# An expert's gather as two rounded-format matmuls, high part and exact rest, in place of one fp32 matmul

## The chip, the cores and the metric

The kernel runs on one core of one Trainium2 chip. The metric is device time in microseconds for one launch; the time before is the median of three runs. The program times each launch as a whole, while the profile comes from one profiled execution.

## The reference

Two residual layers over 256 tokens of width 1024. Layer 0 is a gated linear recurrence beside a dilated attention, then a dense SwiGLU. Layer 1 is a differential attention, then a mixture of experts, and this last stage is what matters here:

```
logits = (xt @ router)                      # 256 tokens x 8 experts
top_v, top_i = lax.top_k(logits, 2)
gates = jax.nn.softmax(top_v, axis=-1)
for e in range(8):
    h = jax.nn.silu(xt @ w1[e]) * (xt @ w3[e])      # 1024 -> 2816
    y = y + dense_gate[:, e:e + 1] * (h @ w2[e])    # 2816 -> 1024
```

Each expert has 34.6 MB of fp32 weights; about a quarter of the tokens choose it.

## The kernel before, in words

All large matmuls are made of three products in a rounded fp32 format that the program calls F32R (and the profile fp32r): a number is split into its high part, rounded to that format, and the exact rest, and hi·hi + hi·lo + lo·hi is summed in PSUM. Weights come in tiles of 1408, 1536 or 1024 columns into eight raw buffers. For each tile ScalarE writes the high part into one of four `whi` buffers (`split_hi`, line 279), VectorE subtracts it from the raw tile to give `wlo` (`split_lo`, line 286), and TensorE runs the three products (`tile_products`, lines 305 to 307). The order on every engine is written out by hand; semaphores join them. SyncE loads a raw buffer again when its `wlo` is done.

The experts run one after the other. For expert n VectorE makes a one-hot matrix `pick` (256 tokens x 128 seats, in two halves of 128 tokens; `pick_tokens`, line 1130) that says which token sits in which seat. TensorE's `gather(n)` (line 1578) then multiplies the tokens with it. For each of KD = 8 chunks of the width and each of NT = 2 halves of the tokens there is one matmul whose stationary operand is 128 tokens x 128 features of `xn` and whose moving operand is the 128 columns of `pick`. These give the expert's input, turned, in PSUM banks 4 and 5. Behind them `gather` transposes `pick` (line 1588, needed to scatter the result back) and multiplies it with the gates (line 1590). ScalarE and VectorE split the gathered input into `xe_hi` and `xe_lo` (`gather_hi`, line 743; `gather_lo`, line 1139), which the expert's up blocks take as stationary operands. `xn` is a plain fp32 copy of x, made once by ScalarE on line 736, because VectorE scales x itself afterwards (line 1218).

`gather(0)` stands on the way into the first expert. The other seven are issued in the middle of the preceding expert, behind its up block 2 (GATHER_AFTER). The up blocks before and behind them need nothing of the gather.

Ahead of `gather(0)` VectorE has, in this order: a copy for the router (line 1098), three `split_lo` of the first expert's tiles, the copy of the router's logits out of PSUM (line 1101), the chain of small operations that ranks them (to line 1128), and `pick_tokens(0, 0)`. TensorE meanwhile computes the logits (line 1565) and, for the seats, a few matmuls of 8 columns (lines 1571 to 1575).

Of the kernel before, what the change touches and what calls it, by code (L numbers as in the profile page):

```python
# [15 lines left out]
ALU = mybir.AluOpType  # L16
ACT = mybir.ActivationFunctionType
AX_X = mybir.AxisListType.X
F32 = mybir.dt.float32
F32R = mybir.dt.float32r  # L20
# [3 lines left out]
P = 128  # L24
S, D = 256, 1024
NT = S // P
# [6 lines left out]
NE = 8  # L33
# [20 lines left out]
G_DN = [[(3, NB)] * 4, [(3, NB), (3, NB), (2, NB), (2, NB)]]  # L54
# [53 lines left out]
def trunk(nc, a, c, out):  # L108

    with ExitStack() as ctx:  # L110
        sem = lambda name: ctx.enter_context(nc.semaphore(name))
# [6 lines left out]
        def at(name, shape, dt=F32, offset=None):  # L118
            size = int(np.prod(shape[1:])) * (1 if dt == U8 else 4)
            here = cur[0] if offset is None else offset  # L120
            if offset is None:
                cur[0] = here + (size + 31) // 32 * 32
            assert here + size <= top, (name, here + size, top)
            return nc.alloc_sbuf_tensor_at(name, shape, dt, offset=here), here + (size + 31) // 32 * 32

        def own(name, shape, dt=F32):
            return at(name, shape, dt)[0]
# [4 lines left out]
        x = own("x", [P, NT, D])  # L132
        xT_at = cur[0]
# [3 lines left out]
        ident, earlier, slots = small[:, 0, :], small[:, 1, :], small[:, 2, :]  # L137
# [11 lines left out]
        gains, after_gains = at("gains", [P, 2, D], F32, phase)  # L149
# [4 lines left out]
        ropeT, _ = at("ropeT", [P, 2, 512], F32, o)  # L154
# [35 lines left out]
        sq0, on0 = four_heads(expE[0]), four_heads(qk2[0])  # L190

        xn, m2 = at("xn", [P, NT, D], F32, after_gains)
        xe_hi, m3 = at("xe_hi", [P, KD, P], F32R, m2)
        xe_lo, m4 = at("xe_lo", [P, KD, P], F32R, m3)
        h_e, m5 = at("h_e", [P, FF], F32, m4)
        hTe_hi, m6 = at("hTe_hi", [P, KF, P], F32R, m5)
        hTe_lo, m7 = at("hTe_lo", [P, KF, P], F32R, m6)
        silu_e, m8 = at("silu_e", [P, 2, NU], F32, m7)
        pick, m9 = at("pick", [P, NT, P], F32, m8)  # L200
        put_next, m10 = at("put_next", [P, S], F32R, m9)
        put, m11 = at("put", [P, S], F32R, m10)
        y_hi, m12 = at("y_hi", [P, D], F32R, m11)
        y_lo, m13 = at("y_lo", [P, D], F32R, m12)
        xT_f, m14 = at("xT_f", [P, KD, S], F32, m5)
        route, m16 = at("route", [P, 12, NT, NE], F32, m13)
        cmp, m17 = at("cmp", [P, 2, NT, NE, NE], F32, m16)
        ones, m19 = at("ones", [P, P], F32, m17)
        seat, m20 = at("seat", [P, NT, 2 * NE], F32, m19)
        gate_col, m21 = at("gate_col", [P, NT], F32, m20)  # L210
        slot_gate, m22 = at("slot_gate", [P, 2], F32, m21)
        more, m23 = at("more", [P, 1], I32, m22)

        late = [at(f"late{j}", [P, kc * n], F32, where)[0] for j, ((kc, n), where) in
                enumerate(zip(G_DN[1], (xT_at, xT_at + 6144, xT_at + 12288, m23)))]

        psum = ctx.enter_context(nc.psum_tensor("psum", [P, 8, 512], F32))

# [22 lines left out]
        rope2_pool = sem("rope2_pool")  # L242
        lam_x = sem("lam_x")
        c_s, c_mx, c_e, c_a, c_tp, c_te, c_av = (sem(n) for n in ("c_s", "c_mx", "c_e", "c_a", "c_tp", "c_te", "c_av"))
        rt_in, bf_in, rx_act, rx_dve, m_lg, m_sel, m_ex, m_d, m_pos, more_set, xn_set = (
            sem(n) for n in ("rt_in", "bf_in", "rx_act", "rx_dve", "m_lg", "m_sel", "m_ex", "m_d", "m_pos", "more_set", "xn_set"))
        m_pick, m_ga, m_ga_hi, m_ga_lo, m_put_r, m_gt, m_cur = (
            sem(n) for n in ("m_pick", "m_ga", "m_ga_hi", "m_ga_lo", "m_put_r", "m_gt", "m_cur"))
        m_silu, m_h, m_tp, m_thi, m_tlo, m_yhi, m_ylo, m_sc, m_acc = (
# [6 lines left out]
        def by_bank(xT, b):  # L256

            return xT[:, 4 * (b % 2):4 * (b % 2) + 4, (b // 2) * P:(b // 2 + 1) * P]
# [22 lines left out]
        def split_lo(dve, q, par, shapes, js=range(GT), in_late=False):  # L281
            for j in js:
                kc, n = shapes[j]
                dve.wait_ge(hi_done, 2 * GT * q + GT * par + j + 1)
                src = late[j] if in_late else raw[GT * par + j]
                nc.vector.tensor_tensor(wlo[j][:, 0:kc * n], src[:, 0:kc * n],  # L286
                                        whi[j][:, 0:kc * n].bitcast(F32), ALU.subtract).then_inc(lo_done, 1)
# [38 lines left out]
        def dn_src(w2, half, part):  # L326
            return [w2[:, k0:k0 + kc, half * NB:(half + 1) * NB] for k0, (kc, _) in zip(DN_K0[part], G_DN[part])]
# [9 lines left out]
        def dn_src_e(e, half, part):  # L337
            return [m_w2[:, bass.ds(e, 1), k0:k0 + kc, half * NB:(half + 1) * NB].rearrange("p e k n -> p (e k) n")
                    for k0, (kc, _) in zip(DN_K0[part], G_DN[part])]

        TURNS = [(0, 4, 6, 3), (4, 4, 7, 4), (8, 4, 6, 5), (12, 4, 7, 6), (16, 3, 6, 7), (19, 3, 3, None)]
        TURN_AFTER = {after: g for g, (_, _, _, after) in enumerate(TURNS) if after is not None}
        GATHER_AFTER = 2

# [15 lines left out]
        def q_moe(n):  # L362

            return Q_MOE + 6 * n
# [186 lines left out]
        def _(act):  # L551
# [181 lines left out]
            for b in range(3):  # L733
                act.wait_ge(t_ps, 20 + b + 1)
                nc.scalar.copy(by_bank(xT_f, b), psum[:, 4 + b, :].rearrange("p (k s) -> p k s", s=P)).then_inc(rx_act, 1)
            nc.scalar.copy(xn[:], x[:]).then_inc(xn_set, 1)
            act.wait_ge(m_d, 1)
            nc.scalar.activation(route[:, 4], route[:, 3], ACT.Exp).then_inc(m_ex, 1)

# [69 lines left out]
        def _(dve):  # L809
            n_link = [0]  # L810

            def link(ins):
                n_link[0] += 1
                ins.then_inc(dve_link, 1)
                dve.wait_ge(dve_link, n_link[0])
# [161 lines left out]
            for t in range(NT):  # L977
                ins = nc.vector.tensor_tensor(proj[:, t, 512:1024].rearrange("p (h c) -> p h c", h=BH),
                                              psum[:, 6 + t, :].rearrange("p (h c) -> p h c", h=BH),
                                              rinv[:, t, :, None].broadcast_to([P, BH, BD]), ALU.mult)  # L980
# [116 lines left out]
            dve.wait_ge(t_ps, 24)  # L1097
            nc.vector.tensor_copy(by_bank(xT_f, 3), psum[:, 7, :].rearrange("p (k s) -> p k s", s=P)).then_inc(rx_dve, 1)
            split_lo(dve, q_moe(0), 0, G_UP, js=(1, 2, 3))
            dve.wait_ge(m_lg, 1)  # L1100
            link(nc.vector.tensor_copy(route[:, LG], psum[:, 0, 0:NT * NE].rearrange("p (t e) -> p t e", e=NE)))

# [143 lines left out]
        def _(pe):  # L1246
# [127 lines left out]
            for b in range(4):  # L1374
                for kk in range(2):
                    for t in range(NT):
                        col = QB + (2 * b + kk) * P
                        ins = nc.tensor.transpose(psum[:, b, kk * S + t * P:kk * S + t * P + P], proj[:, t, col:col + P], ident)
# [4 lines left out]
            for t in range(NT):  # L1383
                for h in range(AH):
                    dst = psum[:, 6 + t, h * AD:(h + 1) * AD]
                    v = [proj[:, tt, VA + h * AD:VA + (h + 1) * AD] for tt in range(NT)]
                    nc.tensor.matmul(dst, ATd[:, t, h, :], v[t], start=True, stop=False)
                    ins = nc.tensor.matmul(dst, ATo[:, h, 1 - t, :], v[1 - t], start=False, stop=True)
# [170 lines left out]
            for t in range(NT):  # L1559
# [4 lines left out]
                for k in range(KD):  # L1564
                    ins = nc.tensor.matmul(psum[:, 0, t * NE:(t + 1) * NE], xT_f[:, k, t * P:(t + 1) * P], router[:, k, :],
                                           start=(k == 0), stop=(k == KD - 1))
# [7 lines left out]
            for t in range(NT):  # L1574
                ins = nc.tensor.matmul(psum[:, 2, 0:NE], ones[:], route[:, SEL, t, :], start=(t == 0), stop=(t == NT - 1))
            ins.then_inc(m_pos, 1)

            def gather(n):

                pe.wait_ge(m_pick, n + 1)  # L1580
                for k in range(KD):
                    for t in range(NT):
                        ins = nc.tensor.matmul(psum[:, 4 + k // 4, (k % 4) * P:(k % 4 + 1) * P],  # L1583
                                               xn[:, t, k * P:(k + 1) * P], pick[:, t, :], start=(t == 0), stop=(t == NT - 1))
                    if k % 4 == 3:
                        ins.then_inc(m_ga, 1)
                for t in range(NT):
                    ins = nc.tensor.transpose(psum[:, 6, 2 * P + t * P:3 * P + t * P], pick[:, t, :], ident)
                for t in range(NT):
                    ins = nc.tensor.matmul(psum[:, 6, 0:1], pick[:, t, :], gate_col[:, t:t + 1],  # L1590
                                           start=(t == 0), stop=(t == NT - 1))
                ins.then_inc(m_gt, 1)

# [27 lines left out]
            def expert(n, last):  # L1621

                q0 = q_moe(n)
                for b in range(1, UB):
                    block_e(n, b)
                    if b == GATHER_AFTER:
                        pe.wait_ge(m_acc, 2 * n + 1)
                        if not last:
                            gather(n + 1)
                    if b in TURN_AFTER:  # L1630
                        g = TURN_AFTER[b]
                        pe.wait_ge(m_h, 8 * n + b + 2)
                        if g == 0 and not last:
                            pe.wait_ge(m_put_r, 2 * n + 4)
                        if g >= 2:
                            pe.wait_ge(m_tlo, 6 * n + g - 1)
                        turn_hidden_e(n, g)
# [18 lines left out]
                scatter(n, 1)  # L1656

            pe.wait_ge(xn_set, 1)
            gather(0)
            pe.wait_ge(more_set, 1)  # L1660
            first_block(0)
# [33 lines left out]
```

## Time and profile before

| | |
|---|---|
| median of 3 runs | 1432.34 us (1428.77 to 1434.25) |
| profiled execution, first to last instruction | 1432.0 us |
| TensorE (PE) busy | 1340.4 us, 94% |
| weight loads (PEld) busy | 1221.9 us, 85% |
| VectorE (DVE) busy | 1095.1 us, 76% |
| ScalarE (ACT) busy | 841.0 us, 59% |
| gather matmuls (line 1583) | 256 records, 32.1 us |
| chain that ended last | TensorE 86%, VectorE 9% |

For the profiled execution only its span is given, 1432.0 us; no time of its own stands beside it. The span is 0.3 us under the median, so a sum made against the span is carried over to the median as it is. A record's duration on TensorE includes the time the pipeline takes to fill and empty, so records overlap: the pace of a row of matmuls is the distance between their starts, not the duration of one. Line 1583 has 128 matmuls in the program (8 experts x 8 chunks x 2 halves) and 256 records: an fp32 matmul appears as two records, each with a weight load of its own. The weight loads and matmuls of the rounded format appear as one record each.

### The profile page before, as it was taken

What the parts mean: (1) busy time and instruction counts of PE and PEld (TensorE: products, weight loads), DVE (VectorE), ACT (ScalarE), POOL (GpSimd) and SP (SyncE); (2) the same over time, 40 slices, a digit from 0 to 9 for tenths busy, and PEclk for the clock granted to TensorE, in tenths of its full rate; (3) what the DMA queues carried; (4) which work ended last, traced back from release to release, by engine and by line L of the source; (5) the groups of instructions that cost most, each with busy time, mean ns of one, the idle gap of its engine ahead of it and who ended that gap; (6) DMA issues with size and microseconds to landing.
All of it is one profiled execution on the core that took longest, in us unless ns stands there. A gap on an engine that the chain in (4) does not pass through costs nothing.

```text
span 1432.0 us, 20794 instructions
## 1 busy us (share of the span) xinstructions
PE 1340.4 (94%) x7430; PEld 1221.9 (85%) x7430; DVE 1095.1 (76%) x1056; ACT 841.0 (59%) x884; POOL 117.3 (8%) x91
## 2 busy tenths in 40 slices
PE   6997898999898976799999999999999999999995
PEld 5887787999686865699899899898998998998994
DVE  4777646444455995669889889989989888898987
ACT  3555333433333463267768767768667677687772
POOL 1044201000001922100000000000000000000001
PEclk9998878999998997799999999999999999999998
DMA  9552025665345531769999999999999999999980
GB/s 331 184 191 68 1 87 175 183 198 188 118 118 178 166 125 25 240 237 329 344 331 347 358 327 346 364 321 342 360 330 346 365 326 347 330 346 355 370 305 31
DMA packets 227056, 359.02 MB, mean 251 GB/s; under 512 B 8400, under 2 KB 155984, under 8 KB 226880
## 3 DMA queue, kind: packets, MB, share of 16 engines
q1 hardware_dynamic: 225344, 351.50, 71.9%
q0 software_dynamic: 1664, 6.88, 1.4%
q8 instruction: 30, 0.49, 0.2%
q14 instruction: 18, 0.15, 0.0%
HBM read 357.30 MB, written 1.05 MB: 250 GB/s over the span
## 4 chain that ended last, share of the span: by engine, by line
PE 86%; DVE 9%; issue 2%; ACT 1%; POOL 1%; DMA 1%; SPq 0%; DVEq 0%; ACTq 0%
PE psum L305 25%; PE psum L307 24%; PE psum L306 24%; DVE wlo L286 3%; PE psum L1583 2%; PE psum L1597 1%; PE psum L1423 1%; DMA raw<-in_ev_w_in 1%; DVE x L837 1%; PE psum L1256 1%; PE psum L1359 1%; PE psum L1339 1%; PE psum L1407 1%; PE psum L1273 1%; PE psum L1399 1%
## 5 line engine op out<-in xcount | busy, mean ns | idle before, releaser
L286 DVE TENSOR_TENSOR wlo<-raw,whi 128x1408 fp32r<-128x1408 f32 (+2 forms) x500 | 794.6, 1608 | 229.4 <-ACT whi L279 224.6
L279 ACT CAST whi<-raw 128x1408 fp32r<-128x1408 f32 (+2 forms) x500 | 661.6, 1328 | 343.5 <-PE psum L307 312.8
L305 PE MATMUL psum<-whi,xe_hi 128*128 128x352 f32 x1024 | 332.4, 325 | 1.3 <-DVE mv L1215 1.3
L307 PE MATMUL psum<-whi,xe_lo 128*128 128x352 f32 x1024 | 330.6, 323 | 0.0
L306 PE MATMUL psum<-wlo,xe_hi 128*128 128x352 f32 x1024 | 330.4, 323 | 0.0
L305 PEld LDWEIGHTS psum<-whi,xe_hi 128*128 128x128 f32 x1024 | 192.4, 188 | 2.0 <-issue 1.4
L305 PE MATMUL psum<-whi,xT_hi 128*128 128x352 f32 (+1 forms) x512 | 186.3, 364 | 8.3 <-DVE wlo L286 6.1
L306 PEld LDWEIGHTS psum<-wlo,xe_hi 128*128 128x128 f32 x1024 | 192.4, 188 | 0.6
L307 PEld LDWEIGHTS psum<-whi,xe_lo 128*128 128x128 f32 x1024 | 192.4, 188 | 0.0
L306 PE MATMUL psum<-wlo,xT_hi 128*128 128x352 f32 (+1 forms) x512 | 185.2, 362 | 0.0
L307 PE MATMUL psum<-whi,xT_lo 128*128 128x352 f32 (+1 forms) x512 | 184.7, 361 | 0.0
L305 PE MATMUL psum<-whi,hTe_hi 128*128 128x512 f32 x352 | 140.6, 399 | 0.0
L306 PE MATMUL psum<-wlo,hTe_hi 128*128 128x512 f32 x352 | 139.3, 396 | 0.0
L307 PE MATMUL psum<-whi,hTe_lo 128*128 128x512 f32 x352 | 139.2, 395 | 0.0
L305 PEld LDWEIGHTS psum<-whi,xT_hi 128*128 128x128 f32 x512 | 98.2, 192 | 20.7 <-issue 6.7
L307 PEld LDWEIGHTS psum<-whi,xT_lo 128*128 128x128 f32 x512 | 98.3, 192 | 10.6
L306 PEld LDWEIGHTS psum<-wlo,xT_hi 128*128 128x128 f32 x512 | 98.3, 192 | 10.1
L451 POOL TENSOR_SCALAR ln_rs<-mv 128x1 f32<-128x1 f32 x8 | 4.9, 612 | 1086.4 <-DVE mv L830 1086.1
L307 PEld LDWEIGHTS psum<-whi,hTe_lo 128*128 128x128 f32 x352 | 66.2, 188 | 15.9
L306 PEld LDWEIGHTS psum<-wlo,hTe_hi 128*128 128x128 f32 x352 | 66.2, 188 | 15.3
L305 PEld LDWEIGHTS psum<-whi,hTe_hi 128*128 128x128 f32 x352 | 66.2, 188 | 15.2
L762 ACT ACTIVATE silu_e<-psum 128x352 f32<-128x352 f32 x64 | 29.7, 464 | 37.6 <-PE psum L307 37.6
(244 smaller groups left out, 1305.3 us busy)
## 6 DMA issues: line engine op xcount, KB each, us to landing
raw<-in_od_w SPq DMA_DIRECT2D x256, 704.0 KB, 6.1
raw<-in_od_w SPq DMA_DIRECT2D x94, 768.0 KB, 6.2
raw<-in_ev_w SPq DMA_DIRECT2D x32, 704.0 KB, 4.2
raw<-in_ev_w_in SPq DMA_DIRECT2D x32, 512.0 KB, 5.4
raw<-in_od_w SPq DMA_DIRECT2D x30, 512.0 KB, 6.1
raw<-in_od_w_in SPq DMA_DIRECT2D x24, 512.0 KB, 3.8
raw<-in_ev_w SPq DMA_DIRECT2D x12, 768.0 KB, 4.5
raw<-in_ev_w_out SPq DMA_DIRECT2D x8, 512.0 KB, 4.4
```

The costliest lines, as they stand in the source:

```text
L279: nc.scalar.copy(whi[j][:, 0:kc * n], src[:, 0:kc * n]).then_inc(hi_done, 1)
L286: nc.vector.tensor_tensor(wlo[j][:, 0:kc * n], src[:, 0:kc * n], whi[j][:, 0:kc * n].bitcast(F32), ALU.subtract).then_inc(lo_done, 1)
L305: nc.tensor.matmul(ps, hi[:, k, t0:t0 + P], w_h, start=(k == first_k), stop=False)
L306: nc.tensor.matmul(ps, hi[:, k, t0:t0 + P], w_l, start=False, stop=False)
L307: last = nc.tensor.matmul(ps, lo[:, k, t0:t0 + P], w_h, start=False, stop=(k == last_k))
L762: nc.scalar.activation(silu_e[:, b % 2, :], psum[:, 2 * (b % 2), 0:NU], ACT.Silu).then_inc(m_silu, 1)
L837: ins = nc.vector.tensor_tensor(v, v, gains[:, 0, :], ALU.mult)
L1256: ins = nc.tensor.transpose(psum[:, 4 + 2 * t + kb, kk * P:(kk + 1) * P], src(4 * kb + kk, t), ident)
L1273: ins = nc.tensor.matmul(ps, lo[:, k, t * P:(t + 1) * P], w_h, start=False, stop=(k == last_k))
L1339: nc.tensor.matmul(dst, lf_hi[:, t, d, h * AD:(h + 1) * AD], m, start=True, stop=False)
L1359: ins = nc.tensor.matmul(dst, k_[:, ts * P:(ts + 1) * P], q_[:, tt * P:(tt + 1) * P], start=True, stop=True)
L1583: ins = nc.tensor.matmul(psum[:, 4 + k // 4, (k % 4) * P:(k % 4 + 1) * P], xn[:, t, k * P:(k + 1) * P], pick[:, t, :], start=(t == 0), sto ...
```

## The change

`xn` becomes two tiles in the rounded format, `xn_hi` (ScalarE's copy on line 736 now writes it) and `xn_lo` (a new subtraction on VectorE, x minus `xn_hi`, 2048 elements in each of 128 partitions). `pick` is held in the rounded format, in which 0 and 1 are exact. `gather` does two matmuls, with `xn_hi` and `xn_lo`, where it did one in fp32. The transposes and the gate matmuls read `pick` as fp32 as before. `cmp` moves to another place in memory, and so does the last of the `late` tiles. TensorE waits once for `xn_lo` before `gather(0)`.

```diff
-        xn, m2 = at("xn", [P, NT, D], F32, after_gains)
+        xn_hi, m2 = at("xn_hi", [P, NT, D], F32R, after_gains)
...
-        pick, m9 = at("pick", [P, NT, P], F32, m8)
+        pick, m9 = at("pick", [P, NT, P], F32R, m8)
...
-        cmp, m17 = at("cmp", [P, 2, NT, NE, NE], F32, m16)
-        ones, m19 = at("ones", [P, P], F32, m17)
+        cmp, _ = at("cmp", [P, 2, NT, NE, NE], F32, m14)
+        ones, m19 = at("ones", [P, P], F32, m16)
...
+        xn_lo, m24 = at("xn_lo", [P, NT, D], F32R, m23)
...
-            nc.scalar.copy(xn[:], x[:]).then_inc(xn_set, 1)
+            nc.scalar.copy(xn_hi[:], x[:]).then_inc(xn_set, 1)
...
             split_lo(dve, q_moe(0), 0, G_UP, js=(1, 2, 3))
+            dve.wait_ge(xn_set, 1)
+            nc.vector.tensor_tensor(xn_lo[:], x[:], xn_hi[:].bitcast(F32), ALU.subtract).then_inc(xn_rest, 1)
             dve.wait_ge(m_lg, 1)
...
                 for k in range(KD):
+                    dst = psum[:, 4 + k // 4, (k % 4) * P:(k % 4 + 1) * P]
                     for t in range(NT):
-                        ins = nc.tensor.matmul(psum[:, 4 + k // 4, (k % 4) * P:(k % 4 + 1) * P],
-                                               xn[:, t, k * P:(k + 1) * P], pick[:, t, :], start=(t == 0), stop=(t == NT - 1))
+                        nc.tensor.matmul(dst, xn_hi[:, t, k * P:(k + 1) * P], pick[:, t, :], start=(t == 0), stop=False)
+                        ins = nc.tensor.matmul(dst, xn_lo[:, t, k * P:(k + 1) * P], pick[:, t, :], start=False, stop=(t == NT - 1))
...
-                    ins = nc.tensor.transpose(psum[:, 6, 2 * P + t * P:3 * P + t * P], pick[:, t, :], ident)
+                    ins = nc.tensor.transpose(psum[:, 6, 2 * P + t * P:3 * P + t * P], pick[:, t, :].bitcast(F32), ident)
...
-                    ins = nc.tensor.matmul(psum[:, 6, 0:1], pick[:, t, :], gate_col[:, t:t + 1],
+                    ins = nc.tensor.matmul(psum[:, 6, 0:1], pick[:, t, :].bitcast(F32), gate_col[:, t:t + 1],
...
             pe.wait_ge(xn_set, 1)
+            pe.wait_ge(xn_rest, 1)
             gather(0)
```

## Rows read from the trace of the kernel before

**Rows 1.** The page: engine, busy us, share of the span, instructions.

```profile
PE 1340.4 (94%) x7430; PEld 1221.9 (85%) x7430; DVE 1095.1 (76%) x1056; ACT 841.0 (59%) x884; POOL 117.3 (8%) x91
```

**Rows 2.** Waits, 634 to 1248 us: who waited for whom, us, times, longest.

```profile
ACT whi L279 <- PE psum L307: 118.1, 164, 2.0
DVE wlo L286 <- ACT whi L279: 71.4, 129, 4.1
ACT silu_e L762 <- PE psum L307: 30.0, 49, 0.6
```

**Rows 3.** Stretches: length, busy per engine, granted clock, DMA share, GB/s.

```profile
634.00:1248.00 614.00, 614.00 (x3574) 575.12 (x3573) 535.65 (x442) 445.89 (x414) 0.00 (x0) 1.00 0.98 344
...
605.20:611.02 5.82, 5.82 (x33) 5.82 (x34) 0.80 (x2) 0.58 (x1) 0.00 (x0) 0.61 0.00 1
...
600.00:605.00 5.00, 2.30 (x10) 2.21 (x10) 3.19 (x19) 0.22 (x1) 0.00 (x0) 0.50 0.92 304
```

**Rows 4.** Timeline around one later gather: start, length, engine, line, operation.

```profile
737.00 3.74 PE L1583 MATMUL psum<-pick,xn 128*128 128x128 f32 x32
...
740.57 0.38 PE L1588 MATMUL psum<-small,pick 128*128 128x128 f32 x2
740.68 0.53 PEld L1590 LDWEIGHTS psum<-gate_col,pick 128*128 128x128 f32 x4
```

**Rows 5.** Timeline of TensorE ahead of the first gather.

```profile
601.24 0.60 PE L1571 MATMUL psum<-route,small 128*128 128x8 f32 x2 [2.76 <-DVE route L1113]
...
602.54 1.00 PE L1575 MATMUL psum<-route,ones 128*128 128x8 f32 x4
605.20 5.98 PE L1583 MATMUL psum<-pick,xn 128*128 128x128 f32 x32 [1.66 <-DVE gate_col L1133]
611.02 0.38 PE L1588 MATMUL psum<-small,pick 128*128 128x128 f32 x2
```

**Rows 6.** Single lines: duration ns minimum/median/maximum, first and last start, forms.

```profile
L1583 PEld LDWEIGHTS psum<-pick,xn x256: 187/192/333, 605.2 to 1244.4; 128*128 128x128 f32 x128
...
L1339 PEld LDWEIGHTS psum<-lev,xT_hi x64: 186/188/333, 113.3 to 148.3; 128*128 128x128 f32 x64
L1339 PE MATMUL psum<-lev,xT_hi x64: 276/280/583, 113.3 to 148.4; 128*128 128x256 f32 x64
...
L1597 PEld LDWEIGHTS psum<-small,h_e x176: 137/139/143, 647.9 to 1384.6; 128*128 128x128 f32 x176
...
L1575 PE MATMUL psum<-route,ones x4: 361/361/361, 602.5 to 603.2; 128*128 128x8 f32 x4
```

**Rows 7.** Timeline, matmuls of 256 columns in the rounded format, first and last.

```profile
116.06 0.41 PE L1339 MATMUL psum<-lev,xT_hi 128*128 128x256 f32 x1
...
117.13 0.41 PE L1340 MATMUL psum<-lev,xT_lo 128*128 128x256 f32 x1
...
147.00 0.28 PE L1339 MATMUL psum<-lev,xT_hi 128*128 128x256 f32 x1
...
148.53 0.28 PE L1340 MATMUL psum<-lev,xT_lo 128*128 128x256 f32 x1
```

**Rows 8.** Timeline, the same format at 512 columns, first and last of 20.

```profile
579.64 0.39 PE L1271 MATMUL psum<-whi,xT_hi 128*128 128x512 f32 x1
...
583.95 0.39 PE L1272 MATMUL psum<-wlo,xT_hi 128*128 128x512 f32 x1
```

**Rows 9.** Groups by line and form, TensorE: busy us, mean ns, idle before.

```profile
L305 PE MATMUL psum<-whi,xe_hi 128*128 128x352 f32 x1024 | 332.4, 325 | 1.3 <-DVE mv L1215 1.3
L305 PE MATMUL psum<-whi,hTe_hi 128*128 128x512 f32 x352 | 140.6, 399 | 0.0
```

**Rows 10.** Timeline of ScalarE, VectorE and TensorE where the new subtraction goes.

```profile
593.72 1.90 ACT L736 COPY xn<-x 128x2048 f32<-128x2048 f32 x1
...
596.24 3.15 DVE L286 TENSOR_TENSOR wlo<-raw,whi 128x1408 fp32r<-128x1408 f32 x2
...
597.70 0.79 PE L1565 MATMUL psum<-router,xT_f 128*128 128x8 f32 x3
...
599.31 0.17 DVE L1101 COPY route<-psum 128x16 f32<-128x16 f32 x1
```

**Rows 11.** Lines of VectorE with the nearest operations: count, busy us, mean ns.

```profile
L910 DVE TENSOR_TENSOR xT_lo<-sA,xT_hi 128x1024 fp32r<-128x1024 f32 x2 | 4.2, 2128 | 0.9 <-ACT xT_hi L606 0.9
L1132 DVE TENSOR_SCALAR pick<-small,seat 128x128 f32<-128x128 f32 x16 | 3.8, 280 | 0.0
L896 DVE TENSOR_TENSOR sB<-sB,lbs 128x2048 f32<-128x2048 f32 x1 | 2.3, 2283 | 0.0
```

More of the change, by code:

```diff
@@ L212, in trunk @@
         more, m23 = at("more", [P, 1], I32, m22)
+        xn_lo, m24 = at("xn_lo", [P, NT, D], F32R, m23)
         late = [at(f"late{j}", [P, kc * n], F32, where)[0] for j, ((kc, n), where) in
-                enumerate(zip(G_DN[1], (xT_at, xT_at + 6144, xT_at + 12288, m23)))]
+                enumerate(zip(G_DN[1], (xT_at, xT_at + 6144, xT_at + 12288, m24)))]
         psum = ctx.enter_context(nc.psum_tensor("psum", [P, 8, 512], F32))
@@ L244, in trunk @@
         c_s, c_mx, c_e, c_a, c_tp, c_te, c_av = (sem(n) for n in ("c_s", "c_mx", "c_e", "c_a", "c_tp", "c_te", "c_av"))
-        rt_in, bf_in, rx_act, rx_dve, m_lg, m_sel, m_ex, m_d, m_pos, more_set, xn_set = (
-            sem(n) for n in ("rt_in", "bf_in", "rx_act", "rx_dve", "m_lg", "m_sel", "m_ex", "m_d", "m_pos", "more_set", "xn_set"))
+        rt_in, bf_in, rx_act, rx_dve, m_lg, m_sel, m_ex, m_d, m_pos, more_set, xn_set, xn_rest = (
+            sem(n) for n in ("rt_in", "bf_in", "rx_act", "rx_dve", "m_lg", "m_sel", "m_ex", "m_d", "m_pos", "more_set", "xn_set", "xn_rest"))
         m_pick, m_ga, m_ga_hi, m_ga_lo, m_put_r, m_gt, m_cur = (
```

## The prediction, written before the changed kernel was run

> **What bounds the kernel now.** I read the page's busy times first. TensorE is busy for 94% of the span, and has as many weight loads as matmuls, 7430 each [rows 1]. So every matmul record brings a load of its own, which matters below. Then the stretch that holds the loop over the experts: in its 614 us TensorE is busy for 614.00, at the full clock [rows 3]. There the other engines wait for TensorE and not the other way round: ScalarE waited 118.1 and 30.0 us for its products, and VectorE 71.4 us for ScalarE [rows 2]. Whatever is added to TensorE's queue inside an expert is added to the time, and whatever is taken out of it comes off, as long as the weights keep coming. The DMA share of 0.98 in that stretch [rows 3] says that large savings would meet the loads; a microsecond or two in an expert's 100 (the stretch holds about six of them) need not. Ahead of the first expert it is otherwise: TensorE is idle for over half of the stretch 600 to 605 [rows 3], because it waits for VectorE's routing chain. There VectorE's time counts.
>
> **Part 1: the gather's matmuls.** One fp32 gather is 16 matmuls and 32 records. They start at 737.00, and the transpose behind them at 740.57, which makes 3.57 us, or 0.112 us a record [rows 4]. The changed gather has 16 x 2 = 32 matmuls. If each is one record, as all of this format are, the count of records doesn't fall: 32 loads and 32 matmuls as before. What each carries falls, if a record of an fp32 matmul of 128 columns streams them twice. Its duration says so: fp32 at 128 columns takes 275 ns (the 3.74 us of the row of 32, less 31 steps of 0.112) [rows 4], about the 280 of the rounded format at 256 columns [rows 6]. So the question is what sets the pace when the streaming gets shorter.
>
> Bounds of the pace of a rounded matmul of 128 columns: from above, what 256 columns of the same format take, at the lower clock and at the full one: 116.06 to 117.13 is 5 steps of 0.214, and 147.00 to 148.53 is 13 steps of 0.118 [rows 7]. From below, what its 128 columns would need if the load hid: half of the fp32 record, 0.056. From further above, 512 columns: 583.95 less 579.64 over 19 steps, 0.227 [rows 8]. I take 0.115, between the fp32 load's 0.113 and the 0.118. A gather is then 32 x 0.115 = 3.68, 0.11 more than now, and seven of them in the loop give +0.8 us. The first gather takes 5.82 us at a mean clock of 0.61, so some 4.5 of them at the lower one [rows 3, 5]; there 256 cycles are the same before and after (0.213 against 0.214), so it gives +0.1 at most. By the ends 0.112 and 0.118 the eight gathers give 0 to +1.6 us.
>
> The Trainium skill has a rule that speaks against such an edit. "TensorE: Matmul & The Clock Gate", section "LDWEIGHTS (loading the stationary operand)", puts the load at the number of its columns over 1.2 GHz, whatever the matmul behind it streams; for 128 that is 107 ns, and by it the gather would be 32 x 0.107 = 3.4 us, within 0.2 of now. The trace agrees at the full clock (0.113) and not at the lower one, where the step is 0.213: there the measurement decides.
>
> **Part 2: the new subtraction on VectorE.** It stands behind three `split_lo` and ahead of the copy of the logits. ScalarE's copy ends at 593.72 + 1.90 = 595.62, so VectorE doesn't wait for it. The logits are there at 598.49; VectorE ends its last split at 599.4 by the rows, which round and overlap a little, and takes the logits at 599.31 [rows 10]. VectorE is thus the late one by 0.8 us already, and everything that it gets here pushes the whole chain: ranking, seats, `pick`, `gather(0)`, first block. The nearest row for 128x2048 is 2283 ns [rows 11]; the `split_lo` just before it, 3.15 us for 2 x 1408 elements [rows 10], gives 2048 x 1.12 = 2.29. A row of 1024 elements took 2128 ns [rows 11], by which it would be 4.3; TensorE and ScalarE stand still here, and I take 2.3. Nothing hides it: TensorE waits for `pick`, and behind it has work at 100% to the end of the loop, so no later slack takes it back. Moved past it on VectorE's queue are only the routing operations.
>
> **The rest.** ScalarE's copy now writes the rounded format, 1.9 us with some 3.7 to spare. `pick` in the rounded format: the 280 ns of rows 11 twice per expert, on VectorE, which in the loop is ahead; only the first two count, between nothing and +0.3 (if writing that format doubled them), and I take 0. The wait for `xn_rest` ends before VectorE even begins the routing, and behind it in TensorE's queue is only `gather(0)`, which waits for `pick` anyway. Transposes, gate matmuls and the copies out of PSUM are unchanged in form and number. The moved tiles cost no time. No DMA is added.
>
> **Sum**, against the span of 1432.0 us: +2.3 (subtraction) +0.8 (seven gathers) +0.1 (the first) = 1435.2; the median is 0.3 above the span, so **1435.5 us**, +0.2%. A difference of less than 0.5% (7 us) is what a measurement of this kernel can't tell from none: its three runs span 5.5 us. Own range of this case, with the pace's ends, the 4.3 for the subtraction and the spread of medians: 1431 to 1440.
>
> **Rival 1, the narrow matmul loses the fast rate** (the side of slower). Each matmul of the rounded format in this program streams 256, 352 or 512 columns, and each narrower one is fp32; none shows what 128 costs. If it streams at the rate of true fp32, it takes four times 128 cycles, like 512 columns: 0.227 each [rows 8], so 32 x 0.227 = 7.26 us, 3.69 more. Seven give +25.8. The first has 4.5 us at the lower clock, enough for 10 or 11 of twice 0.213, and 21 or 22 at 0.227 behind them: 9.4 against 5.8, +3.6. With 2.3 that is +31.7: 1464. It would be about the same if each were issued as two records like fp32 (64 x 0.112 = 7.2): 1463. It decides from a pace of 0.131 up, where 256 x 0.019 = 4.9 us and the 2.3 make half a per cent. For it speaks only that such a matmul is avoided everywhere; against it, that durations fall on a line with the columns: 399, 325, 280 ns for 512, 352 and 256 [rows 9, 6], 0.46 ns a column, with no sign of a step down to 256. Chance 0.25.
>
> **Rival 2, the gather is nearly halved.** If the load of this format can follow at 128 cycles, or hides, the pace is 0.056 to 0.060: a gather of 1.9 us, 1.7 less; seven give -11.7, the first -2.4 at most, with the subtraction -11.8: 1420.5. The change counts on this. For it: the load's duration of 188 ns holds a latency that the trace doesn't part from its occupancy, and in the program's other places the pace of loads is hidden under wider matmuls. Against it: the equal durations at two clocks. Chance 0.10.
>
> Beside this rival stands the same page of the Trainium skill, section "Weight-path perf modes — Fast Weight Load (FWL) and DoubleRow": loads of 128 columns in a type that isn't FP32 are read several elements at a time. If the rounded type counted as such, the time would be rival 2's; the trace's equal durations speak against it.
>
> **Rival 3, the subtraction costs nothing** because VectorE isn't late or the chain has slack, with part 1 as forecast: 1433.2. It is inside the first case's range; chance 0.03, counted with it.
>
> **How the numbers follow.** Forecast 0.62 with rival 3 another 0.03; rival 1 0.25; rival 2 0.10. The predicted time is the first's. Holding 8 in 10 needs rival 1 and leaves out rival 2: 1430 to 1466. Faster by over 0.5%: rival 2, 0.10, and 0.01 of chance spread. Slower by over 0.5%: rival 1's 0.25 and 0.04 of the forecast's case with a subtraction or pace at its upper end. Within: 0.60.
>
> **What the changed profile would show.** 256 records on the gather's two lines, 128 each, and 7430 matmuls in all (rival 1 in its second form: 256 more). The distance from the first gather matmul to the transpose behind it: 3.6 to 3.8 us in my case, about 7.2 in rival 1, about 1.9 in rival 2. The duration of one such matmul near 220 ns (280 less 128 x 0.46) where it streams its columns once. A subtraction of 2.3 us on VectorE right ahead of the logits' copy, and the idle time of TensorE before the seats' matmuls up from 2.8 [rows 5] to about 5 us. If the loop gets longer in places other than the gather, or TensorE shows idle time in it, the prediction is wrong in what it takes for the bound.

## The result and the profile after

The changed kernel took 1437.41 us (median of 6 runs, 1433.81 to 1441.42), the kernel before 1432.11 beside it (6 runs): a ratio of 1.0042, 95% interval 1.0024 to 1.0060, or +6.0 us with +3.4 to +8.6. Measured again in the experiments it was 1.0034 (1.0022 to 1.0046), +4.9 us. The forecast was +3.2.

The busy times first, as [rows 1]. The count of matmuls and loads is unchanged; TensorE is even 3 us less busy.

```profile
PE 1337.3 (93%) x7430; PEld 1219.1 (85%) x7430; DVE 1096.7 (77%) x1057; ACT 840.8 (59%) x884; POOL 117.2 (8%) x91
```

The timeline of one later gather, to be held against [rows 4]: the first and last of its 32 matmuls, and the transposes behind them.

```profile
737.09 0.22 PE L1587 MATMUL psum<-pick,xn_hi 128*128 128x128 f32 x1
737.14 0.28 PE L1588 MATMUL psum<-pick,xn_lo 128*128 128x128 f32 x1
...
740.49 0.28 PE L1588 MATMUL psum<-pick,xn_lo 128*128 128x128 f32 x1
740.61 0.41 PE L1592 MATMUL psum<-small,pick 128*128 128x128 f32 x2
```

It takes 740.61 - 737.09 = 3.52 us instead of 3.57. Only the first matmul shows the short duration of 0.22 us; the fp32 gather has no record under 0.272 in any place. The other 31 last about 0.28 although they stream as few columns as the first: those 31, whose starts are a load apart (3.52 / 32 = 0.110), hold some waiting too. Of the 0.05 us only about half reaches the next products. The starts of the next gather show it:

```profile
837.88 0.22 PE L1587 MATMUL psum<-pick,xn_hi 128*128 128x128 f32 x1
```

```profile
837.82 3.74 PE L1583 MATMUL psum<-pick,xn 128*128 128x128 f32 x32
```

From one gather to the next it is 100.79 us in the changed kernel and 100.82 (from 737.00) in the kernel before: 0.03 less an expert, 0.2 for seven.

The timeline from the new subtraction to the first gather, on into the first block and to the last matmul, beside [rows 5, 10]. The brackets give how long the engine stood idle before, and for whom:

```profile
588.70 1.90 ACT L737 CAST xn_hi<-x 128x2048 fp32r<-128x2048 f32 x1
...
594.28 2.28 DVE L1102 TENSOR_TENSOR xn_lo<-x,xn_hi 128x2048 fp32r<-128x2048 f32 x1
596.48 0.17 DVE L1104 COPY route<-psum 128x16 f32<-128x16 f32 x1
...
598.41 0.59 PE L1574 MATMUL psum<-route,small 128*128 128x8 f32 x2 [4.95 <-DVE route L1116]
...
602.37 0.45 PE L1587 MATMUL psum<-pick,xn_hi 128*128 128x128 f32 x1 [1.65 <-DVE gate_col L1136]
...
611.65 0.63 PE L306 MATMUL psum<-whi,xe_hi 128*128 128x352 f32 x1 [1.14 <-DVE mv L1218]
...
1416.95 0.40 PE L1611 MATMUL psum<-y_lo,put 128*128 128x512 f32 x1
```

The last matmul of the kernel before:

```profile
1417.02 0.40 PE L1607 MATMUL psum<-y_lo,put 128*128 128x512 f32 x1
```

And stretches with TensorE's granted clock (the column behind the five engines; 1.00 is 2.4 GHz and 0.50 is 1.2 GHz): the loop, the whole time at the lower clock, the first gather, and the start of the first block. The second fence has the kernel before, where the block started at 1.00.

```profile
634.00:1248.00 614.00, 614.00 (x3576) 575.28 (x3575) 535.62 (x442) 446.01 (x415) 0.00 (x0) 1.00 0.98 344
...
584.30:614.95 30.65, 21.08 (x92) 20.40 (x93) 17.07 (x38) 4.21 (x7) 1.38 (x3) 0.50 0.51 178
...
602.37:609.22 6.85, 6.85 (x32) 6.85 (x33) 0.80 (x2) 0.59 (x1) 0.00 (x0) 0.50 0.00 0
...
611.65:614.90 3.25, 3.25 (x11) 3.25 (x12) 0.89 (x1) 0.00 (x0) 0.00 (x0) 0.50 0.00 0
```

```profile
589.30:609.70 20.40, 14.16 (x65) 13.54 (x65) 12.10 (x30) 3.19 (x4) 1.38 (x3) 0.50 0.77 269
...
613.07:616.30 3.23, 3.23 (x20) 3.23 (x21) 0.88 (x1) 0.99 (x1) 0.00 (x0) 1.00 0.00 0
```

Stage by stage, profile after against profile before (from starts of records): ScalarE's copy of x to the first gather 13.67 us against 11.48, +2.19, the subtraction. The first gather itself 6.85 against 5.82 [rows 3]; from its start to the first block's first product 9.28 against 7.87, +1.41. From there to the last matmul 805.30 against 803.95, +1.35. That is +1.53 in the first block (its 18th matmul starts 4.32 us behind the first instead of 2.79; 11 start in the first 3.25 us where there were 20), and -0.18 behind it, in the seven later gathers. The sum is +4.95. The two spans are equal all the same, because the profile after came to ScalarE's copy 5.0 us sooner (588.70 against 593.72): in the stages ahead, which the change doesn't touch, the same 2732 matmuls kept TensorE busy for 518.86 us where they took 524.85, at a mean granted clock of 0.93 against 0.92. Differences of this kind are in every run, so the medians count and the profiles are compared by stage.

### The profile page after: what moved, and what is told of

It reads as the page before. It is cut to its first block, busy times and chain, and to the rows that moved or that the text cites. A ratio compares the mean times of both kernels' runs of the same rounds, so it can differ in the third digit from the quotient of the medians.

```text
span 1431.9 us, 20795 instructions
## 1 busy us (share of the span) xinstructions
PE 1337.3 (93%) x7430; PEld 1219.1 (85%) x7430; DVE 1096.7 (77%) x1057; ACT 840.8 (59%) x884; POOL 117.2 (8%) x91
## 4 chain that ended last, share of the span: by engine, by line
PE 86%; DVE 9%; issue 2%; ACT 1%; POOL 1%; DMA 1%; SPq 0%; DVEq 0%; ACTq 0%
PE psum L306 25%; PE psum L308 24%; PE psum L307 24%; DVE wlo L287 3%; PE psum L1601 1%; PE psum L1588 1%; PE psum L1587 1%; DMA raw<-in_ev_w_in 1%; PE psum L1426 1%; PE psum L1362 1%; DVE x L838 1%; PE psum L1402 1%; PE psum L1410 1%; PE psum L1276 1%; PE psum L1275 1%
## 5 line engine op out<-in xcount | busy, mean ns | idle before, releaser
L308 PEld LDWEIGHTS psum<-whi,hTe_lo 128*128 128x128 f32 x352 | 66.3, 188 | 15.9
```

Source lines behind the costliest of these rows:

```text
L308: last = nc.tensor.matmul(ps, lo[:, k, t0:t0 + P], w_h, start=False, stop=(k == last_k))
```

## Experiments

**The change again**, on the chip of the next three.

> The changed kernel once more, beside the others on one chip. If its excess is what its own profile shows against the one of before (19.35 us from ScalarE's copy of x to the first block became 22.95, and another 1.3 us of the first block ran at the lower clock), it is 4 to 6 us slower than before. If only the subtraction's 2.3 us counts and the rest was chance in the clock, it is 2 to 3 us slower.

Measured: 1434.79 us against 1431.07, ratio 1.0034 (1.0022 to 1.0046), +4.9 us. Its profile has the same three stages as the first one, within 0.03 (13.67, 9.29, 805.27). The excess is more than the subtraction.

**The subtraction alone**, in the kernel with the fp32 gather.

```diff
+            dve.wait_ge(xn_set, 1)
+            nc.vector.tensor_tensor(xn_lo[:], x[:], xn[:], ALU.subtract).then_inc(xn_rest, 1)
             dve.wait_ge(m_lg, 1)
...
+            pe.wait_ge(xn_rest, 1)
             gather(0)
```

> The kernel before with VectorE's subtraction in its place and the gather left in fp32 (the subtraction's result isn't used). Theory A, that the whole cost is the subtraction on the routing chain and what it does to TensorE's clock: as slow as the changed kernel, +4 to +6 us, the first gather wholly at granted clock 0.5 and near 6.9 us long. Theory B, that the two matmuls in the rounded format cost part of it: +2.3 us, the first gather as before, 5.8 us.

Measured: 1433.34, ratio 1.0016 (1.0007 to 1.0025), +2.3 us. Theory B's number. A stretch of its profile, the first gather in fp32:

```profile
606.68:612.74 6.06, 6.06 (x33) 6.06 (x34) 0.80 (x2) 0.59 (x1) 0.00 (x0) 0.58 0.00 0
...
614.79:618.00 3.21, 3.21 (x20) 3.21 (x21) 0.89 (x1) 0.95 (x1) 0.00 (x0) 1.00 0.00 0
```

TensorE had stood idle the same 4.96 us ahead of the seats as in the changed kernel, and yet its clock rose within the gather (some 0.5 us later into it than before, so 6.06 us instead of 5.82), and the first block ran at full clock.

**The two matmuls alone**, without the subtraction; the exact rest is left out of the gathered values.

```diff
-            dve.wait_ge(xn_set, 1)
-            nc.vector.tensor_tensor(xn_lo[:], x[:], xn_hi[:].bitcast(F32), ALU.subtract).then_inc(xn_rest, 1)
...
-                        ins = nc.tensor.matmul(dst, xn_lo[:, t, k * P:(k + 1) * P], pick[:, t, :], start=False, stop=(t == NT - 1))
+                        ins = nc.tensor.matmul(dst, xn_hi[:, t, k * P:(k + 1) * P], pick[:, t, :], start=False, stop=(t == NT - 1))
```

> The changed kernel without the subtraction: the second product of the gather reads the high part again, so the rest is left out and the number of matmuls stays. Theory A: within 1 us of before, each later gather 3.5 us from its first matmul to the transposes as before (3.57). Theory B: 2 to 3 us slower than before.

Measured: 1436.31, ratio 1.0035 (1.0020 to 1.0049), +5.0 us. Theory A fell: the matmuls alone already cost about what the whole change costs, though each later gather takes 3.52 us. Theory B was right in kind and short in size: it expected 2 to 3 us. The idle time ahead of the seats is the 2.75 us of before, and the clock still doesn't rise in the gather:

```profile
606.37:613.23 6.86, 6.86 (x33) 6.86 (x33) 0.80 (x2) 0.59 (x1) 0.00 (x0) 0.50 0.00 0
615.66:620.70 5.04, 5.04 (x18) 5.04 (x19) 0.88 (x1) 1.09 (x1) 0.00 (x0) 0.52 0.00 0
```

These four cases (with and without the subtraction, fp32 and rounded) put the clock down to the gather's matmuls and not to the longer wait. Nor is it the chance of one execution: in all seven profiles that reach a rounded first gather with the clock low (this one, the changed kernel twice, and rates, hidden, between and wide below) it lasts 6.85 or 6.86 us at 0.50, and in both with an fp32 one the clock rises 4.5 to 5.1 us in. Over all runs beside each other the mean granted clock was 0.959 before (24 runs), 0.958 with the subtraction alone (12), 0.956 in the changed kernel (11) and 0.954 here (8). The new theory A: rounded matmuls of 128 columns behind a low clock leave it low.

**The rates of rounded matmuls**, rows of them added behind each gather into bank 7.

```diff
+                for i in range(16):
+                    nc.tensor.matmul(psum[:, 7, 0:64], xn_hi[:, 0, 0:P], pick[:, 0, 0:64], start=True, stop=True)
+                for i in range(16):
+                    nc.tensor.matmul(psum[0:64, 7, 0:P], xn_hi[:, 0, 0:64], pick[:, 0, :], start=True, stop=True)
...
+                for i in range(8):
+                    nc.tensor.matmul(psum[:, 7, 0:512], xn_hi[:, 0, 0:P], xn_hi[:, 0, 0:512], start=True, stop=True)
+                    nc.tensor.matmul(psum[:, 7, 0:P], xn_hi[:, 0, 0:P], pick[:, 0, :], start=True, stop=True)
```

> The changed kernel with rows of matmuls in the rounded format added behind each gather, into a bank that nobody reads: 16 each of stationary columns x moving columns 128x64, 64x128, 64x64, 64x256, 128x256, and 8 pairs of 128x512 and 128x128. Theory L, the weight load sets the pace (256 cycles for 128 columns, 0.111 us; streaming is one column a cycle): 128x64 at 0.111, 64x128 at 0.056 to 0.07 if the load goes by its columns, 64x64 at 0.056, and a pair of 512 and 128 at 0.227 + 0.056 = 0.28. Theory S, streaming below 256 columns takes two cycles a column: 128x64 at 0.056, 64x128 at 0.111, and the pair at 0.227 + 0.111 = 0.34.

Measured, by the start of each row of matmuls in the timeline behind the second gather (stationary columns stand behind the star, moving columns behind the x):

```profile
653.00 0.47 PE L1593 MATMUL psum<-pick,xn_hi 128*128 128x64 f32 x3
...
654.76 0.25 PE L1595 MATMUL psum<-pick,xn_hi 128*64 128x128 f32 x1
...
655.75 0.25 PE L1597 MATMUL psum<-pick,xn_hi 128*64 128x64 f32 x2
...
656.65 0.31 PE L1599 MATMUL psum<-pick,xn_hi 128*64 128x256 f32 x1
...
658.51 0.28 PE L1601 MATMUL psum<-pick,xn_hi 128*128 128x256 f32 x1
...
660.42 0.40 PE L1603 MATMUL psum<-xn_hi 128*128 128x512 f32 x1
660.66 0.22 PE L1604 MATMUL psum<-pick,xn_hi 128*128 128x128 f32 x1
...
663.05 0.22 PE L1604 MATMUL psum<-pick,xn_hi 128*128 128x128 f32 x1
663.11 0.28 PE L1606 MATMUL psum<-small,pick 128*128 128x128 f32 x1
```

Sixteen of each: 128x64 in 1.76 us, 0.110 each; 64x128 in 0.99, 0.062; 64x64 in 0.90, 0.056; 64x256 in 1.86, 0.116; 128x256 in 1.91, 0.119. Halving the streaming changes nothing while the load is 128 columns wide, and halving the load brings 128 moving columns down to 0.062. That is theory L: the load takes two cycles a column, the streaming one. Theory S is out. But the pair of 512 and 128 took 2.69 / 8 = 0.336 us, where L said 0.28. Read with the single rows: 0.227 + 0.109. The load for the next 512-column matmul doesn't begin before the 128-column one (L1604) starts at 660.66, as the loads of the first pairs show; one load is ahead and no more:

```profile
660.43 0.19 PEld L1604 LDWEIGHTS psum<-pick,xn_hi 128*128 128x128 f32 x1
660.66 0.19 PEld L1603 LDWEIGHTS psum<-xn_hi 128*128 128x128 f32 x1
```

The same rows stand behind the first gather, and there they bear on the clock. First the granted clock from the gather's start, and from just after its rise; then the rows:

```profile
603.29:619.18 15.89, 15.89 (x91) 15.89 (x92) 1.50 (x3) 1.17 (x2) 0.00 (x0) 0.50 0.00 0
619.30:621.80 2.50, 2.50 (x24) 2.50 (x22) 0.00 (x0) 0.00 (x0) 0.00 (x0) 1.00 0.00 0
```

```profile
610.15 3.56 PE L1593 MATMUL psum<-pick,xn_hi 128*128 128x64 f32 x16
613.53 1.95 PE L1595 MATMUL psum<-pick,xn_hi 128*64 128x128 f32 x16
615.27 1.85 PE L1597 MATMUL psum<-pick,xn_hi 128*64 128x64 f32 x16
616.94 3.11 PE L1599 MATMUL psum<-pick,xn_hi 128*64 128x256 f32 x16
```

TensorE was busy for 15.9 us without a gap and stayed at the lower clock, as long as its rounded matmuls streamed 128 or 64 columns; the clock rose 2.3 us into the row that streams 256. So the rounded format as such doesn't keep the clock low. It is one profile, and in that row the loads are narrower too.

**The subtraction hidden** behind `pick`, with the 16 products of the high part first in the first gather.

```diff
             nc.vector.tensor_scalar(more[:], ...).then_inc(more_set, 1)
+            dve.wait_ge(xn_set, 1)
+            nc.vector.tensor_tensor(xn_lo[:], x[:], xn_hi[:].bitcast(F32), ALU.subtract).then_inc(xn_rest, 1)
...
+                for part in range(2):
+                    if part:
+                        pe.wait_ge(xn_rest, 1)
+                    for k in range(KD):
...
```

> The changed kernel with the subtraction behind the seats and pick on VectorE; the first gather does all 16 products of the high part first and those of the rest behind them, so that the subtraction lies beside the former. Theory A (subtraction on the routing chain +2.2 us; rounded matmuls keep TensorE's clock low through the first gather and into the first block, +2.8 us or more): 2.2 us faster than the changed kernel, +2.5 to +3.5 us against before, with the first gather still 6.9 us at granted clock 0.5. Theory B (the clock is low because TensorE idles 2.2 us longer): the first gather gets its clock back within it, 5.8 us, and the time is that of before within 1 us.

Measured: 1434.86 against 1432.03, ratio 1.0027 (1.0016 to 1.0038), +3.9 us. Theory A's first gather:

```profile
603.51:610.37 6.86, 6.86 (x33) 6.86 (x33) 3.00 (x3) 0.59 (x1) 0.00 (x0) 0.50 0.00 0
612.80:618.50 5.70, 5.70 (x19) 5.70 (x20) 1.17 (x2) 1.36 (x1) 0.00 (x0) 0.50 0.00 0
```

The 2.2 us are gone from the stage ahead of the gather (11.47 again), but the first block now runs 5.7 us at the lower clock instead of 3.3 and gives back 1.1 of them (806.43 from its first product to the last matmul, against 805.30). So the two costs don't add: what the chain saves, the clock takes back in part. That makes the stages' sum +3.9, a little over the 2.5 to 3.5 expected. The other profiles repeat it: the block's stretch at the lower clock is 3.3 to 3.5 us long where the subtraction stands on the chain (the changed kernel twice, wide) and 4.8 to 5.8 us where it doesn't (no_sub, between, this one). In all six the whole time at the lower clock, from its fall 4 to 5 us ahead of ScalarE's copy, is the same 30.7 us.

**TensorE kept streaming in the routing**, in the kernel before and in the changed one. The cut shows the former; the latter has busy(8, 1) in place of busy(5, 1), three more for its longer wait.

```diff
+            def busy(n, bank):
+                for i in range(n):
+                    nc.tensor.matmul(psum[:, bank, 0:3 * P], ident, small[:].rearrange("p a b -> p (a b)"), start=True, stop=True)
...
             for t in range(NT):
+                busy(2, 6)
                 transpose_chunks(x_chunk, ts=(t,), norm=2)
+                busy(1, 1 if t else 6)
...
+                    if k == 3:
+                        busy(1, 1)
...
             SEL = 5
+            busy(5, 1)
             pe.wait_ge(m_sel, 1)
...
             ins.then_inc(m_pos, 1)
+            busy(2, 3)
...
             gather(0)
+            busy(1, 7)
```

> The kernel before with fp32 matmuls of 384 columns added on TensorE, on a constant and into banks that nobody reads, where it waits in the routing or streams only 8 columns a load. If the low clock there costs time: the first gather 3.6 us instead of 5.8, the router's matmuls twice as fast, 3 to 5 us faster than before. If the added matmuls only delay the chain: 1 to 3 us slower.

> The same matmuls added to the changed kernel (three more in the longer wait). Theory A: with the clock up when the gather begins, the rounded gather takes 3.5 us like the later ones, and the cost against warm_before shrinks to the subtraction's, +2.2 less 0.4 for the gathers; against before 1 to 3 us faster. Theory B', that the rounded gather is slow at first for a reason of its own: the first gather stays near 6.9 us and the time at least 2 us above before.

Measured: the kernel before with them 1426.62, ratio 0.9966 (0.9954 to 0.9977), -4.9 us; the changed kernel with them 1431.00, 0.9988 (0.9977 to 0.9999). Their first gathers, fp32 and then rounded:

```profile
600.44:604.09 3.65, 3.65 (x33) 3.65 (x34) 0.80 (x2) 0.59 (x1) 0.00 (x0) 1.00 0.17 62
```

```profile
601.90:605.50 3.60, 3.60 (x33) 3.60 (x33) 0.80 (x2) 0.59 (x1) 0.00 (x0) 1.00 0.00 0
```

With the clock up, the rounded gather is as fast as the fp32 one, here too; theory B' is out. The profiles differ by +2.19 (subtraction), -0.05 (first gather) and -0.16 (first block to last matmul), +2.0 in all, while the ratios' middles differ by 0.0022, 3.1 us. With the clock up the change is left with its subtraction, within what these runs can tell.

**The gather spread between wider products**: its 32 matmuls one by one between the products of up block 3.

```diff
+                    if between is not None:
+                        between(4 * j + kk, 0)
                     last = nc.tensor.matmul(ps, lo[:, k, t0:t0 + P], w_h, start=False, stop=(k == last_k))
...
+                    if between is not None:
+                        between(4 * j + kk, 1)
```

> The kernel with the hidden subtraction, and the later seven gathers taken apart: their 32 matmuls of 128 columns stand one by one between the 352-column products of up block 3. Theory L1 (a matmul costs the longer of its own streaming and the NEXT matmul's load, one load ahead; the measured pair of 512 and 128 columns took 0.336 us): each still costs 0.109, no gain, within 1.5 us of hidden. Theory L2 (loads run ahead by several matmuls, so that only columns and loads summed over a stretch count): each costs 0.056 to 0.067, 10 to 12 us faster than hidden.

Measured: ratio 1.0027 (1.0017 to 1.0037), the same as hidden. One turn of its timeline, three products of 352 and two of 128 columns:

```profile
742.18 0.38 PE L306 MATMUL psum<-whi,xe_hi 128*128 128x352 f32 x1
742.39 0.32 PE L307 MATMUL psum<-wlo,xe_hi 128*128 128x352 f32 x1
742.55 0.22 PE L1643 MATMUL psum<-pick,xn_hi 128*128 128x128 f32 x1
742.61 0.38 PE L310 MATMUL psum<-whi,xe_lo 128*128 128x352 f32 x1
742.83 0.22 PE L1643 MATMUL psum<-pick,xn_lo 128*128 128x128 f32 x1
742.89 0.38 PE L306 MATMUL psum<-whi,xe_hi 128*128 128x352 f32 x1
```

0.71 us a turn; less three products at 0.160 that is 0.115 for each narrow one. The one behind starts only 0.06 later, as if the narrow one were cheap, but then needs 0.21 or 0.22 to the next instead of 0.16: it had to wait for its load. Theory L1.

**Fewer loads**: `pick` stationary, the tokens' two parts streaming 512 columns, then 8 transposes; alone, and with the hidden subtraction and the streaming in the routing.

```diff
+                for half in range(2):
+                    for t in range(NT):
+                        for part in (xn_hi, xn_lo):
+                            ins = nc.tensor.matmul(psum[:, 4 + half, :], pick[:, t, :], part[:, t, half * NB:(half + 1) * NB],
+                                                   start=(t == 0 and part is xn_hi), stop=(t == NT - 1 and part is xn_lo))
...
+                        nc.scalar.copy(rows_e.rearrange("p (b s) -> p b s", b=2), psum[:, 4:6, :]).then_inc(m_gx, 1)
...
+                        for k in range(KD):
+                            ins = nc.tensor.transpose(psum[:, 4 + k // 4, (k % 4) * P:(k % 4 + 1) * P],
+                                                      rows_e[:, k * P:(k + 1) * P], ident)
```

> The changed kernel with the seven later gathers turned over: pick is the stationary operand and 512 columns of the high part and of the rest stream past it, 8 matmuls instead of 32; ScalarE copies the rows out, and 8 transposes behind up block 4 turn them. If a matmul costs the longer of its own streaming and the next one's load, a gather is 8 x 0.227 + 8 x 0.110 = 2.7 us of TensorE instead of 3.5: 5 to 6 us faster than the changed kernel, about the time of before. If ScalarE's added copy (some 1.1 us an expert) makes TensorE wait, up to 8 us slower than that.

> The same with the subtraction behind pick, as in the run named hidden, and with the matmuls of 384 columns in the routing, as in warm_before. If the three effects add up: routing clock -5 us and gathers -5.6 us against a base of before -0.4, the first gather 3.5 us: 1421 to 1424 us, faster than before (about 1432) and than warm_before (1426.6). If the effects overlap, no faster than warm_before.

Measured: wide 1429.79 against 1430.33, ratio 0.9999 (0.9988 to 1.0011); wide_warm 1423.52, 0.9944 (0.9928 to 0.9960), -8.0 us. The later gather and ScalarE's copy in the timeline of wide:

```profile
737.14 0.40 PE L1612 MATMUL psum<-xn_hi,pick 128*128 128x512 f32 x1
...
738.77 0.39 PE L1612 MATMUL psum<-xn_lo,pick 128*128 128x512 f32 x1
...
739.00 0.38 PE L1600 MATMUL psum<-small,pick 128*128 128x128 f32 x2
...
739.20 1.01 ACT L775 COPY h_e<-psum 128x1024 f32<-128x1024 f32 x1
```

Eight matmuls take 739.00 - 737.14 = 1.86 us; from the first block to the last matmul it is 799.76 us, 5.5 less than in the changed kernel, with the low clock in the first block kept. wide_warm beats both kernels. Its middle is also lower than that of warm_before (0.9944 against 0.9966), but the intervals, 0.9928 to 0.9960 and 0.9954 to 0.9977, overlap, so this lead isn't shown. Its first gather took 4.20 us (602.97 to 607.17) and not the 3.5 expected: TensorE stood idle for 0.39 us until the hidden subtraction was done.

```profile
605.33 2.00 PE L1624 MATMUL psum<-pick,xn_lo 128*128 128x128 f32 x16 [0.39 <-DVE xn_lo L1217]
```

## Why the prediction was right, and where it fell short

The number was right within its range, and partly by luck: two of the three terms were off, the later gathers by 1.0 us too much and the first gather by 2.8 too little.

**What bounds the kernel** held: TensorE is busy 614 of 614 us in the loop again, and wide, which takes some 5.5 us out of its queue there, was about that much faster than the changed kernel (0.9999 against 1.0034).

**Seven gathers, +0.8 us**: right in kind. The pace is set by the load, 3.52 us a gather, just under the 3.6 to 3.8 of the forecast's signs; the seven gave -0.2. The sign of a duration near 220 ns showed in the first matmul of a gather only. The step from equal load durations to equal load cost is shown by the rates (0.110 for 64 and for 128 moving columns). Rival 1, four times slower, and rival 2, nearly half, are both out. The rule in the Trainium skill, "TensorE: Matmul & The Clock Gate", section "LDWEIGHTS (loading the stationary operand)", that a load costs by its columns and not by what streams behind it, is borne out: 0.110 with 128 stationary columns, 0.056 with 64. Its figure holds at the full clock only; at the lower one a step of the gather is 6.85 / 32 = 0.214.

**The subtraction, +2.3 us**: right. 2283 ns on VectorE right ahead of the logits' copy, 2.19 in the stage, +2.3 (1.0 to 3.6) alone.

**The first gather, "+0.1 at most"**: this term failed. I wrote that at the lower clock 256 cycles are the same before and after, which is so (0.213), and took for granted that the clock would rise at the same point. It rose within the fp32 gather, about 4.5 us into it, and not within the rounded one, which was busy by the profile's measure all along but streams half as many cycles between the same loads. It rose 3.3 us into the first block. The gather's 5.82 became 6.85, the stage 1.41 longer, and the block lost another 1.53. Instead of +0.1 the term is +2.94, and in the run without the subtraction (no_sub), where the block's low stretch is longer, the stages give +3.4. With the others the sum is 2.19 + 2.94 - 0.18 = 4.95, against a measured 4.9 and 6.0. Nothing in the forecast's list of signs named the clock.

Two readings in it are slightly off, and nothing rests on them. The "four fp32 matmuls of 8 columns" are two matmuls of two records each; the step of 0.213 us is one record's. And 3.74 us less 31 steps of 0.112 is 268 ns, not 275; 275 is the median of the trace's records.

What stays open: why no_sub, at +3.4 by its stages, measured +5.0 (its interval, +2.9 to +7.0, holds both), and how much streaming the clock asks for. That it follows the streaming, and not the format as such, is the nearest reading of the four cases and of the rows behind the first gather of rates, where rounded matmuls of 256 columns raised it after 13.7 us of shorter ones had not. A rounded gather with streams twice as long in its own place was not tried.

## What to carry to other kernels

Count a chain of matmuls by max(its streaming, the next weight load), each in cycles: a format that halves the streaming of 128-column matmuls saves nothing when each has a 128-column load of its own, not even between wider ones. It pays once the operands are turned so that fewer loads stand before longer streams. And where TensorE works in short pieces behind a wait, look at the granted clock from the wait to the first full block: an edit that leaves every duration the same can still move the point at which the clock rises.

## What the runs showed of the hardware that was not expected

- A rounded-format load takes two cycles a stationary column at both clocks (0.110 us for 128 at the full one, 0.211 to 0.214 at the lower), as fp32 does (0.113 and 0.213).
- Only one load runs ahead: a pair of 512 and 128 columns takes 0.336 us and not 0.28.
- The profile's busy share doesn't show what the clock follows. TensorE was 100% busy in the first gather of both fp32 profiles and all seven rounded ones that began at the lower clock; it rose in the former (mean 0.61 and 0.58) and not in the latter (0.50). In rates it stayed low for 15.9 us of busy TensorE from the gather's start.
- Matmuls whose results nobody reads, put into TensorE's waits in one 20 us stage, made the kernel before 4.9 us faster.
